# Memory values of the cross attention by seven half-size products per half, with the operand sums on GpSimd

## What is computed

```python
def cross_attention(h, mem_n, w_q, w_kv, w_o):
    q = (h @ w_q).reshape(B, S, X_HEADS, X_HEAD_DIM)
    k, v = jnp.split(mem_n @ w_kv, 2, axis=-1)
    ...
    s = jnp.einsum('bqhd,bmhd->bhqm', q, k).astype(jnp.float32) / math.sqrt(X_HEAD_DIM)
    p = jax.nn.softmax(s, axis=-1)
    o = jnp.einsum('bhqm,bmhd->bqhd', p.astype(v.dtype), v).reshape(B, S, D_MODEL)
    return o @ w_o
```

## Time and profile before

| | us |
|---|---|
| median of 3 runs | 1742.18 |
| lowest, highest | 1741.54, 1742.64 |
| profiled execution | 1740.04 |
| its span | 1738.2 |
| TensorE busy in the span | 1564.5 |
| VectorE busy | 841.7 |
| ScalarE busy | 377.2 |
| GpSimd busy | 2.2 |

### The profile page before, as it was taken

One profiled execution on the slowest core, in us unless ns is written; L12 is line 12 of the kernel. 1 busy time (PEld: TensorE's weight loads), 2 busy tenths in 40 slices (PEclk: granted clock), 3 DMA queues, 4 the chain that ended last, 5 costly groups with the idle time before them and its releaser, 6 DMA issues.

```text
span 1738.2 us, 26463 instructions
## 1 busy us (share of the span) xinstructions
PE 1564.5 (90%) x10938; PEld 1090.1 (63%) x10938; DVE 841.7 (48%) x1699; ACT 377.2 (22%) x952; POOL 2.2 (0%) x6
## 2 busy tenths in 40 slices
PE   9999999999999999999999999999999756656655
PEld 5877888884488787888648778999854212112111
DVE  6676567665577765765646578564522000000001
ACT  4362131110225422311002571111211000000001
POOL 0000000000000000000000000000000000000000
PEclk9999999999999999999999999999999888677788
DMA  9324335444542242543543322121898999999998
GB/s 394 130 74 157 134 122 211 156 183 169 203 173 97 80 188 73 190 190 146 194 176 146 114 104 77 73 76 51 335 390 358 427 425 424 424 425 425 422 423 332
DMA packets 50050, 386.37 MB, mean 222 GB/s; under 512 B 5648, under 2 KB 6160, under 8 KB 10384
## 3 DMA queue, kind: packets, MB, share of 16 engines
q1 hardware_dynamic: 47952, 375.16, 54.3%
q10 hardware_dynamic: 1984, 9.57, 1.4%
HBM read 383.65 MB, written 1.05 MB: 221 GB/s over the span
## 4 chain that ended last, share of the span: by engine, by line
PE 74%; DMA 19%; DVE 3%; ACT 2%; SPq 2%; issue 1%; DVEq 0%; ACTq 0%
PE ps L239 53%; DMA arena<-in_stream 7%; DMA par<-in_stream 7%; DMA ring<-in_stream 4%; PE ps L2399 3%; PE ps L1127 2%; PE ps L1625 2%; DMA const<-in_stream 1%; PE ps L243 1%; PE ps L1226 1%; PE ps L776 1%; PE ps L1286 1%; PE ps L1259 1%; SPq L3833 1%; SPq L3801 1%
## 5 line engine op out<-in xcount | busy, mean ns | idle before, releaser
L239 PE MATMUL ps<-arena 128*128 128x256 f32 (+4 forms) x2364 | 524.4, 478 | 77.8 <-DMA arena<-in_stream 66.9
L239 PEld LDWEIGHTS ps<-arena 128*128 128x128 f32 (+1 forms) x2364 | 307.5, 171 | 255.9 <-issue 115.4
L239 PE MATMUL ps<-ring,arena 128*128 128x256 f32 (+5 forms) x1172 | 326.0, 517 | 40.6 <-DMA ring<-in_stream 35.4
L239 PEld LDWEIGHTS ps<-ring,arena 128*128 128x128 f32 (+1 forms) x1172 | 179.3, 177 | 161.4 <-issue 80.5
L239 PE MATMUL ps<-arena,ring 128*128 128x256 f32 (+1 forms) x1140 | 235.5, 354 | 0.0
L239 PEld LDWEIGHTS ps<-arena,ring 128*128 128x128 f32 x1140 | 191.2, 191 | 29.0 <-issue 9.6
L3080 DVE TENSOR_TENSOR arena<-arena,ps 128x512 f32<-128x512 f32 x8 | 5.5, 688 | 300.4 <-PE ps L2858 300.4
L2858 PE MATMUL ps<-arena 128*32 128x512 f32 x218 | 132.8, 735 | 0.0
L1174 ACT ACTIVATE arena<-arena,small 128x256 f32<-128x256 f32 x112 | 55.7, 498 | 58.4 <-DVE small L1161 42.0
L239 PE MATMUL ps<-arena,spare 128*128 128x128 f32 x510 | 65.5, 278 | 0.0
L239 PEld LDWEIGHTS ps<-arena,spare 128*128 128x128 f32 x510 | 60.4, 192 | 0.7
(11 more groups left out here) (476 smaller groups left out, 2024.7 us busy)
## 6 DMA issues: line engine op xcount, KB each, us to landing
ring<-in_stream SPq DMA_DIRECT2D x131, 1024.0 KB, 5.0
arena<-in_stream SPq DMA_DIRECT2D x111, 1024.0 KB, 15.4
arena<-in_stream SPq DMA_DIRECT2D x24, 2048.0 KB, 36.4
ring<-in_stream SPq DMA_DIRECT2D x12, 2048.0 KB, 31.8
spare<-in_stream SPq DMA_DIRECT2D x5, 2048.0 KB, 39.2
par<-in_stream SPq DMA_DIRECT2D x8, 1024.0 KB, 38.2
const<-in_stream SPq DMA_DIRECT2D x8, 1024.0 KB, 38.5
spare<-in_stream SPq DMA_DIRECT2D x6, 1024.0 KB, 8.2
```

What stands on the lines that cost most here:

```text
L239: ins = self.pe.e.matmul(out, lhsT, rhs, start=start, stop=stop)
```

## The change

A half of the values (256 tokens x 1024 times 1024 x 512) is cut into quarters: tokens by 128 and the inner dimension by 512, weights by 512 and the columns by 256. Seven products of four 128x256 matmuls each (28) take the place of 16 matmuls of 512 columns. They fill four banks in place of two. The two units of a half are held together and freed together. The sums that the products need are four of weight quarters (128 x 1024 columns each) per half and four of token quarters (128 x 512) once per layer; GpSimd makes them. The weight sums of the first half wait for its two units and for the last bank of the earlier projection that uses the same memory (`spare`); the token sums wait for ScalarE's last copy before the output projection (`out_columns`), since they lie in memory that the self-attention reads; the weight sums of the second half wait for its two units and for the first half's last product. TensorE waits for GpSimd's count before its third product. ScalarE copies the first product of a half out of PSUM; VectorE makes the values from the banks by five additions in place of two copies. The host lays the value weights out in pairs of units.

```diff
+VALUE_MM = 28
+VALUE_X = {0: 5, 1: 5, 2: 7, 3: 11}
-MEMORY_NORM = 32
-MEMORY_X = {0: 6, 1: 6, 2: 8, 3: 12}
...
+def value_pair_pe(p, pe, w, l, half, first, n):
...
+    for r in range(first, first + n):
+        i, k = divmod(r, KC // 2)
...
+        if k == 0 and i == 2:
+            pe.e.wait_ge(p.sem("pool_steps"), VALUE_SUMS * l + (8 if half == 0 else 12))
+        bank = p.value_banks[(0, 0, 1, 2, 2, 3, 3)[i]]
+        out, left, right = ((bank[:, 0, :], a11, b11), (bank[:, 1, :], a12, b21), (bank[:, 0, :], s2, t2), (bank[:, 0, :], s1, t1),
+                            (bank[:, 1, :], s3, t3), (bank[:, 0, :], s4, b22), (bank[:, 1, :], a22, t4))[i]
+        last = k == KC // 2 - 1
+        full = last and i in (1, 2, 4, 6)
+        ins = (pe.e.matmul if full else w.mm)(out, left[:, k, :], right[:, k, :], start=k == 0, stop=last)
...
+        if r == VALUE_MM - 1:
+            w.used(2)
...
+def value_sums_pool(p, pool, l):
...
+    for half in range(2):
+        units = []
+        for v in range(p.mark[f"values{half}_unit"], p.mark[f"values{half}_unit"] + 2):
+            pool.e.wait_ge(p.slot_loaded[v % SLOTS], p.stream_base + 16 * (v // SLOTS + 1))
+            units.append(p.slots[v % SLOTS])
+        pool.e.wait_ge(p.dve_tiles.full, p.mark["values0" if half else f"qk{QK_UNITS - 1}"])
+        b11, b12, b21, b22 = weight_quarters(units)
+        pool.e.tensor_tensor(t1, b12, b11, ALU.subtract).then_inc(pool.step(), 1)
+        pool.e.wait_ge(pool.steps, pool.n)
+        pool.e.tensor_tensor(t2, b22, t1, ALU.subtract).then_inc(pool.step(), 1)
+        pool.e.tensor_tensor(t3, b22, b12, ALU.subtract).then_inc(pool.step(), 1)
+        pool.e.wait_ge(pool.steps, pool.n - 1)
+        pool.e.tensor_tensor(t4, b21, t2, ALU.subtract).then_inc(pool.step(), 1)
+        if half:
+            continue
+        pool.e.wait_ge(p.act_tiles.drained, p.mark["out_columns"])
+        pool.e.tensor_tensor(s1, a21, a22, ALU.add).then_inc(pool.step(), 1)
+        pool.e.wait_ge(pool.steps, pool.n)
+        pool.e.tensor_tensor(s2, s1, a11, ALU.subtract).then_inc(pool.step(), 1)
+        pool.e.tensor_tensor(s3, a11, a21, ALU.subtract).then_inc(pool.step(), 1)
+        pool.e.wait_ge(pool.steps, pool.n - 1)
+        pool.e.tensor_tensor(s4, a12, s2, ALU.subtract).then_inc(pool.step(), 1)
...
+def value_rows_dve(p, dve, half):
...
+    dve.e.tensor_tensor(tile[:, 0, 0:S], first, products[:, 1, :], ALU.add).then_inc(p.dve_tiles.drained, 1)
...
+    dve.e.tensor_tensor(u2, first, products[:, 0, :], ALU.add).then_inc(p.dve_tiles.drained, 1)
...
+    dve.e.tensor_tensor(u, spread(u2, 1, 2), products, ALU.add).then_inc(dve.step(), 1)
...
+    dve.e.tensor_tensor(tile[:, 1, S:2 * S], u[:, 1, :], products[:, 0, :], ALU.add).then_inc(p.dve_tiles.drained, 1)
...
+    dve.e.tensor_tensor(shaped(flat(tile)[:, S:3 * S], 2, S), u, products, ALU.add).then_inc(p.dve_tiles.drained, 1)
...
-    memory_fill_pe(p, pe, w, MEMORY_NORM)
+    value_pair_pe(p, pe, w, l, 0, 0, VALUE_MM)
...
-        memory_fill_pe(p, pe, w, MEMORY_X.get(t, 0))
-        if t == max(MEMORY_X):
-            p.mark["memory_values"] = p.dve_tiles.opened
+        value_pair_pe(p, pe, w, l, 1, p.value_mm, VALUE_X.get(t, 0))
+        p.value_mm += VALUE_X.get(t, 0)
...
+            for l in range(DEPTH):
+                p.stage = f"layer_{l}"
+                value_sums_pool(p, pool, l)
```

More of the change, by code:

```diff
@@ L116 @@
 TOKENS = {"qk": 0, "out": 4, "xq": 8, "xo": 12, "ffn": 16}
-COPIED = {"qk": 0, "out": 4, "xq": 6, "xo": 10, "ffn": 12}
+COPIED = {"qk": 0, "out": 4, "values0": 6, "xq": 7, "values1": 11, "xo": 12, "ffn": 14}
 QK_GAINED = {0: 0, 2: 2, 3: 4}
@@ L939, in first_buffers @@
     p.xkT = p.take(KC, S)
-    p.xv = p.take(NB, D)
+    p.xv = p.take(2, NB, 512)
     assert p.at >= first_mla + 2 * 4 * 1024
@@ L999, in first_buffers @@
     p.pair_junk = p.arena[:, first_pr + NB * D:first_pr + NB * D + 1024]
+    p.value_tokens = [shaped(p.arena[:, first_mla + 512 * n:first_mla + 512 * n + 512], KC // 2, P) for n in range(3)]
+    p.value_tokens.append(shaped(flat(p.qk)[:, KC * S:KC * S + 512], KC // 2, P))
+    p.value_sums = [shaped(p.spare[:, 1024 * n:1024 * n + 1024], KC // 2, S) for n in range(4)]
+    p.value_first = [p.arena[:, at:at + S] for at in (first_pr + NB * D, mark + 4096)]
+    assert first_mla + 1536 <= first_mla + NB * 416 + NB * 384
     def split(sums, tokens, rest):
@@ L1028 @@
 SCALE = {"gqa": 64 ** -0.5, "diff": 1.0, "swa": 1.0, "mla": 96 ** -0.5, "x": 256 ** -0.5}
-MEMORY_UNITS = 8
+KEY_UNITS = 4
 MEMORY_HEADS = {**{t: 3 for t in range(20)}, 20: 2, 21: 2}
-MEMORY_NORM = 32
-MEMORY_X = {0: 6, 1: 6, 2: 8, 3: 12}
+VALUE_MM = 28
+VALUE_X = {0: 5, 1: 5, 2: 7, 3: 11}
+VALUE_SUMS = 12
 DIFF_SQUARES, DIFF_ROOTS, DIFF_ROWS = 15, 20, 21
 MLA_COLUMNS, SWA_COLUMNS, DIFF_COLUMNS = 0, 2, 6
[L1039 to L1044, removed]
 def memory_fill_pe(p, pe, w, n):
-    for u, o in memory_parts(p.memory_mm, n):
+    for r in range(p.memory_mm, min(p.memory_mm + n, KEY_UNITS * UNIT_MM)):
+        o = r % UNIT_MM
+        c, k = divmod(o, KC)
         tiles = p.dve_tiles
@@ L1052, in memory_fill_pe @@
             p.memory_weights = w.next()
[L1053 to L1069, removed]
+            if tiles.opened >= tiles.size:
+                pe.e.wait_ge(tiles.drained, tiles.opened - tiles.size + 1)
+            p.memory_bank = tiles.open(pe)
+        last = o == UNIT_MM - 1
+        ins = (pe.e.matmul if last else w.mm)(p.memory_bank[:, c * S:(c + 1) * S], p.memory_weights[:, o * P:(o + 1) * P],
+                                              p.memgT[:, k, :], start=k == 0, stop=k == KC - 1)
         if last:
             ins.then_inc(tiles.full, 1)
-        if o == (UNIT_MM - 1 if u < 4 else UNIT_MM - 2):
             w.used()
@@ L1077, in memory_fill_dve @@
 def memory_fill_dve(p, dve, n):
-    for u, o in memory_parts(p.memory_seen, n):
-        if u < 4 and o == UNIT_MM - 1:
+    for r in range(p.memory_seen, min(p.memory_seen + n, KEY_UNITS * UNIT_MM)):
+        u, o = divmod(r, UNIT_MM)
+        if o == UNIT_MM - 1:
             dve.e.wait_ge(p.dve_tiles.full, p.dve_tiles.turn(dve))
@@ L1083, in memory_fill_dve @@
             dve.e.tensor_copy(p.xkT[:, 2 * u:2 * u + 2, :], shaped(bank, 2, S)).then_inc(p.dve_tiles.drained, 1)
[L1084 to L1088, removed]
-    p.memory_seen += n
+    p.memory_seen += n
+def value_pair_pe(p, pe, w, l, half, first, n):
+    a11, a12, a21, a22 = quarters(p.memgT)
+    s1, s2, s3, s4 = p.value_tokens
+    t1, t3, t2, t4 = p.value_sums
+    tiles = p.dve_tiles
+    for r in range(first, first + n):
+        i, k = divmod(r, KC // 2)
+        if r == 0:
+            p.mark[f"values{half}_unit"] = w.n
+            p.value_weights, p.value_banks = [w.next() for _ in range(2)], []
+        b11, b12, b21, b22 = weight_quarters(p.value_weights)
+        if k == 0 and i in (0, 2, 3, 5):
+            if tiles.opened >= tiles.size:
+                pe.e.wait_ge(tiles.drained, tiles.opened - tiles.size + 1)
+            p.value_banks.append(shaped(tiles.open(pe), 2, S))
+        if k == 0 and i == 2:
[6 more added lines that the diff above has]
+        ins = (pe.e.matmul if full else w.mm)(out, left[:, k, :], right[:, k, :], start=k == 0, stop=last)
+        if full:
+            ins.then_inc(tiles.full, 1)
+        if r == VALUE_MM - 1:
+            w.used(2)
+            p.mark[f"values{half}"] = tiles.opened
@@ new lines, in value_first_act, with bank @@
+def value_first_act(p, act, half):
+    act.e.wait_ge(p.dve_tiles.full, p.mark[f"values{half}"] - 3)
+    bank = p.dve_tiles.banks[(p.mark[f"values{half}"] - 4) % p.dve_tiles.size]
+    act.e.activation(p.value_first[half], bank[:, 0:S], ACT.Copy).then_inc(act.event("first_copied"), 1)
+def value_rows_dve(p, dve, half):
+    tile, first, u2, u = p.xv[:, half], p.value_first[half], p.pair_shared, p.pair_middle
+    def bank():
+        dve.e.wait_ge(p.dve_tiles.full, p.dve_tiles.turn(dve))
+        return shaped(p.dve_tiles.take(dve), 2, S)
+    products = bank()
+    dve.e.wait_ge(p.sem("first_copied"), COPIED[f"values{half}"] + 1)
+    dve.e.tensor_tensor(tile[:, 0, 0:S], first, products[:, 1, :], ALU.add).then_inc(p.dve_tiles.drained, 1)
+    products = bank()
+    dve.e.tensor_tensor(u2, first, products[:, 0, :], ALU.add).then_inc(p.dve_tiles.drained, 1)
+    dve.e.wait_ge(p.dve_tiles.drained, p.dve_tiles.taken["dve"])
+    products = bank()
+    dve.e.tensor_tensor(u, spread(u2, 1, 2), products, ALU.add).then_inc(dve.step(), 1)
+    dve.e.wait_ge(dve.steps, dve.n)
+    dve.e.tensor_tensor(tile[:, 1, S:2 * S], u[:, 1, :], products[:, 0, :], ALU.add).then_inc(p.dve_tiles.drained, 1)
+    products = bank()
+    dve.e.tensor_tensor(shaped(flat(tile)[:, S:3 * S], 2, S), u, products, ALU.add).then_inc(p.dve_tiles.drained, 1)
@@ L1281, in values_pe @@
         bank = p.act_tiles.open(pe)
[L1282 removed]
+        pe.e.wait_ge(p.dve_tiles.drained, p.mark["values1"])
         for c in range(2):
```

(2 more changed lines are left out.)

19 lines of the change are left out of this document (14 added, 5 removed).

## The result

| | before | after |
|---|---|---|
| median, us | 1742.41 (4 runs) | 1771.41 (4 runs) |
| lowest, highest | 1741.54, 1742.95 | 1767.99, 1774.40 |
| profiled execution | 1740.04 | 1774.40 |
| its span | 1738.2 | 1772.6 |

The ratio is 1.0167, 95% interval 1.0154 to 1.0180: the change costs 29 us. The forecast was 1754, range 1735 to 1763. The direction was right, the size was not.

What follows compares the result with a forecast made beforehand. TensorE was taken as the bound in both layers. Terms -6.5 + 10.4 + 0.6 + 7.0 = +11.5 us on the profiled 1740.04 gave 1751.5, then 1753.7 against the runs' median, say 1754; range 1735 to 1763.

Steps and rivals of the forecast that it cites:

- The bound: TensorE bounds both layers, without slack, so each microsecond off its queue counts and each wait is lost.
- Fewer columns: TensorE's value products take 12.1 us per half instead of 13.73; over two halves and two layers -6.5 us.
- VectorE and ScalarE beside it, slots: Five VectorE additions, ScalarE's extra copy per half and the later freeing of weight units cost nothing.
- over 30 us to spare: Both deadlines of GpSimd's sums, the first and second half's, were said to have this much slack.
- GpSimd's sums: Each sum of 1024 columns was taken as two passes, 1.9 us, and 0.95 for 512 columns.
- What they do to VectorE: While a GpSimd sum is under way, VectorE instructions of certain kinds wait until it ends.
- no interaction: Rival: VectorE and GpSimd run beside each other freely, leaving only the -6.5 us, 1735.7; chance 0.28.
- tensor_scalar going free: Rival: only two-input VectorE instructions are held, so the self-attention costs about 1 us per layer; 1745, chance 0.15.
- Place one: Self-attention: the first half's four weight sums hold VectorE, TensorE waits 5.2 us per layer, +10.4 for two.
- Place two: Output projection: GpSimd's token sums may go before VectorE's; 0.3 us taken per layer, +0.6 for two.
- Place three: Query projection: the second half's sums hold VectorE's token sums; TensorE waits 2.65 and 0.8, 3.5 per layer, +7.0.
- The 1773: Upper end left out of the range: GpSimd's sums at the full three passes, 2.8 us.

Runs made afterwards that it cites:

- e1: Changed kernel without GpSimd's sums, the seven products taking plain quarters (values are other numbers): 1739.36 us against 1742.10, ratio 0.9985.
- e4: Changed kernel with weight sums moved behind VectorE's last weight sums: first half's in the output projection, second half's in the query projection; 1737.51 us, ratio 0.9977.
- e8: The kernel of e4 unchanged, timed in more rounds: 1738.86 us against 1741.53, ratio 0.9981.
- e2: Changed kernel with only the first half's weight sums on GpSimd moved behind VectorE's last weight sums of the output projection: 1749.19 us, ratio 1.0041.
- e5: Changed kernel with the first half's four weight sums spread, waiting for VectorE's 12th, 14th, 16th and 18th scaled probabilities: 1756.83 us, ratio 1.0081.

## Why the prediction was wrong

- **The bound.** "each that it is made to wait is lost": right. The 22.8 us of waits all reach the second block, none is won back.
- **Fewer columns, -6.5.** Right. The value stretch at the norm went from 13.73 to 12.09 us (169.45 to 181.54); e1 arrives 6.1 us early. In the whole time of e1, e4 and e8 only 2.7 to 4.6 us can be seen. Where the rest is given back, behind the layers, isn't settled: their stretch to the experts is 2.1 to 2.3 us longer in the traces, but the trace of before comes from an execution 2.4 under its own median. In the traces of all kernels with the seven products this stretch takes 371.1 (e2) to 376.1 us, and its stage of small matmuls (L2399 before) 120.7 to 123.4 for 119.6 before.
- **VectorE and ScalarE beside it, slots.** Right, nothing: the wait on the last addition is 0.4 as before, and no new wait in the layers names a transfer. GpSimd's deadlines were met, as the prediction had it, though its "over 30 us to spare" for both doesn't follow from its own 176.5 and 203 for the second half.
- **GpSimd's sums, 1.9 us.** Mis-sized: 2.34 to 2.39 for 1024 columns, 1.27 for 512 where nothing delays them. Two passes priced from the memset's row were too low; 2.25, the estimate from the Trainium skill (GPSIMD Engine Reference, section Performance versus the Vector engine), was nearer.
- **What they do to VectorE.** Right in kind: the hold is real and lasts the whole instruction. Both rivals that denied it fall, no interaction (1735.7) by the result, and tensor_scalar going free (1745) by L1267 and L1270.
- **Place one, 5.2 a layer.** This step failed in size. "of which I let VectorE hide 0.5 each under work that isn't held" was wrong: VectorE had reached a held instruction 0.11 us after the first sum began, and then four held ones followed each other (L1267, twice L1270, L1279), none with free work between. I had left the two-column L1267 out of the list. The path was another too: the prediction looked for the wait at the next scores, behind the maxima; TensorE waited a step earlier, at the turning of the probabilities, for the difference L1279, which is held itself. Before, the difference ended at 107.65 and the turning began at 108.21, a slack of 0.56; 8.2 us of holds less that is 7.6, and TensorE came 7.7 late (7.5 of it idle time). Nothing was hidden.
- **The clock.** This step was missing. I priced a wait as its own length. Behind 7.5 us TensorE worked at the lower level, 3.1 us more (2.5 in layer 1), and 2.8 more behind the 3.6 us wait in layer 0; 8.4 us in all, the largest error of the sum.
- **Place two, 0.3 a layer.** 0.1. VectorE's three token sums took 5.14 us for 2.14, but the slack took it.
- **Place three, 3.5 a layer.** Right in place and mechanism, and in size partly by luck. The prediction had two waits, 2.65 and 0.8, from sums of 1.9 us; the first measured 3.6 in both layers, from sums of 2.35 and 2.8. The second, 0.7, stands only in layer 1: in layer 0 TensorE, at the lower clock, came late enough to the third sum.
- **The sum.** With the measured sizes, by starts: -6.4, 15.3 (place one), 0.2, 8.7 (place three), 8.4 (clock), so 26.2 for the 26.1 us of the layers; the forecast had 11.5. The range ended at 1763 because no case held the clock. The 1773 that it left out lies near the result, but it stood for sums of 2.8 us, and they took 2.35 in place one: including it would have been luck.

## What to carry to other kernels

Before work goes to GpSimd, list the VectorE instructions beside the new place by where their inputs lie: those with two inputs in SBUF and fast tensor_scalar from SBUF to SBUF, down to two columns, wait until the GpSimd sum under way has ended, those that read PSUM don't; by where GpSimd's sums stood the same change gained 3 to 5 us or lost 29. Price a new wait of TensorE in a stretch without breaks at more than its length (by the clock behind it 6.4 us cost 2.0 more here, 7.5 us 2.5 and 3.1, 3.6 us 2.8 or nothing), and spread holds that can't be avoided.

## What the runs showed of the hardware that was not expected

- The clock's answer to a wait of 3.6 us differs. Behind it, at the token sums of layer 0, the granted clock was 0.50 in the changed kernel (from 190 us), in e2 (from 178) and in e5 (from 181). In layer 1 it fell in e2 (0.62 from 638.5 to 641) and in e5 (0.63 from 641 to 644), and in the changed kernel it stayed at 1.00; what decides it isn't shown:

```profile
658.50:661.00 2.50, 1.80 (x16) 1.60 (x16) 2.46 (x2) 0.28 (x1) 1.90 (x1) 1.00 0.00 0
```

- The two don't pay alike here. A GpSimd sum with VectorE waiting lasts 2.35 to 2.39 us, the one that first had to let a 512-column VectorE instruction pass 2.79, 0.4 more, while VectorE's went from 0.69 to more than 2.
- GpSimd and VectorE take turns, one instruction each, also where GpSimd's next sum had no semaphore to wait for (from its second sum to its third).
